# Router products on the residual sums; the last tile normalised by ScalarE and GpSimd

## The reference

```python
h = layer_norm(DEEPNORM_ALPHA * h + mix, ln1_g, ln1_b)      # mix: output projection of the mixers
# in the mixture of experts, t is h:
g_logits = t @ router_group_w + router_group_b              # 4 groups
g_idx    = top-1 of softmax(g_logits)
e_logits = t @ router_expert_w + router_expert_b            # 32 experts, 8 in a group
e_top    = top-2 of the chosen group's 8 logits, softmax over them, times the group's probability
hid = silu(t @ exp_w_gate[e]) * (t @ exp_w_up[e])           # 1024 -> 256
out = sum over the two chosen experts of weight * (hid @ exp_w_down[e])
h = layer_norm(DEEPNORM_ALPHA * h + out, ln2_g, ln2_b)
```

## Time and profile before

| | us |
|---|---|
| median of three runs | 458.99 |
| the three runs | 458.12, 458.99, 464.22 |
| profiled execution, whole time | 459.7 |
| its span | 457.5 |
| TensorE busy in the span | 417.1 (91%) |
| VectorE, ScalarE, GpSimd busy | 187.8, 107.4, 84.9 |

### The profile page before, as it was taken

The page is one execution under the profiler, slowest core; times in us unless marked ns, Lnnn a source line. Parts: engine busy times, 40 slices in busy tenths (PEclk is TensorE's granted clock), DMA queues, the critical chain, the costliest instruction groups (busy, mean ns, idle before and its releaser), DMA issues.

```text
span 457.5 us, 6658 instructions
## 1 busy us (share of the span) xinstructions
PE 417.1 (91%) x2588; PEld 283.4 (62%) x2588; DVE 187.8 (41%) x372; ACT 107.4 (23%) x175; POOL 84.9 (19%) x116
## 2 busy tenths in 40 slices
PE   7999999999999999779999999998887897889792
PEld 6888766888888888655555555554455554444330
DVE  2579322999654585762122222222121121120085
ACT  3442447741150014101111111111010010111311
POOL 2500000000000003061333322333112201012033
PEclk9999999999999999989999999999898899989997
DMA  8956322023479999396999999999999999998483
GB/s 293 278 166 215 100 92 94 1 92 94 133 283 389 413 419 381 127 398 222 416 406 409 409 408 409 411 410 409 413 410 413 408 414 414 415 414 349 152 339 142
DMA packets 44480, 139.09 MB, mean 304 GB/s; under 512 B 5288, under 2 KB 15560, under 8 KB 40359
## 3 DMA queue, kind: packets, MB, share of 16 engines
q1 hardware_dynamic: 38288, 126.89, 71.5%
q0 software_dynamic: 6144, 11.84, 7.0%
q10 hardware_dynamic: 22, 0.02, 0.0%
HBM read 134.41 MB, written 12.58 MB: 321 GB/s over the span
## 4 chain that ended last, share of the span: by engine, by line
PE 65%; DMA 18%; SPq 8%; DVE 4%; issue 2%; ACT 1%; DVEq 0%; POOL 0%; POOLq 0%
DMA wgu<-in_exp_w_up 15%; PE bank L1047 14%; PE bank L878 11%; PE bank L879 11%; PE bank L880 11%; PE bank L1066 7%; SPq L494 4%; SPq L490 2%; SPq L491 2%; PE bank L1037 2%; PE bank L1057 2%; PE bank L930 2%; DMA xg<-h_rows,x_rows 1%; DMA pair_y<-y_pairs 1%; PE bank L861 1%
## 5 line engine op out<-in xcount | busy, mean ns | idle before, releaser
L1047 PE MATMUL bank<-wgu,xTg 128*64 128x256 f32 x992 | 121.7, 401 | 19.1 <-DMA wgu<-in_exp_w_up 16.3
L1047 PEld LDWEIGHTS bank<-wgu,xTg 128*64 128x64 f32 x992 | 75.7, 144 | 56.5 <-issue 15.2
L1423 DVE TENSOR_TENSOR hid<-gated,bank 64x256 f32<-64x256 f32 x32 | 13.5, 423 | 132.7 <-ACT gated L811 132.6
L878 PE MATMUL bank<-xT_hi,w_hi 128*128 128x512 f32 x160 | 62.8, 393 | 1.4 <-DVE w_lo L1156 1.4
L879 PE MATMUL bank<-xT_lo,w_hi 128*128 128x512 f32 x160 | 62.3, 390 | 0.0
L880 PE MATMUL bank<-xT_hi,w_lo 128*128 128x512 f32 x160 | 62.3, 389 | 0.0
L652 POOL DMA_INDIRECT y_pairs<-ys,y_rows x32 | 32.3, 1011 | 161.2 <-PE bank L1037 103.8
L1066 PE MATMUL bank<-wdn,hidT 128*64 128x512 f32 x248 | 58.8, 593 | 0.9 <-issue 0.9
L811 ACT ACTIVATE gated<-bank 64x256 f32<-64x256 f32 x32 | 12.1, 377 | 161.7 <-PE bank L1047 161.7
L1142 DVE TENSOR_TENSOR w_lo<-raw,w_hi 128x2048 fp32r<-128x2048 f32 x12 | 27.5, 2290 | 33.1 <-ACT w_hi L726 32.9
L726 ACT ACTIVATE w_hi<-raw 128x2048 fp32r<-128x2048 f32 x12 | 23.0, 1920 | 59.9 <-PE bank L880 52.3
(11 more groups left out here) (237 smaller groups left out, 429.9 us busy)
## 6 DMA issues: line engine op xcount, KB each, us to landing
wgu<-in_exp_w_gate SPq DMA_DIRECT2D x31, 1024.0 KB, 16.0
wgu<-in_exp_w_up SPq DMA_DIRECT2D x31, 1024.0 KB, 21.5
wdn<-in_exp_w_down SPq DMA_DIRECT2D x31, 1024.0 KB, 21.0
raw<-in_w_in SPq DMA_DIRECT2D x9, 1024.0 KB, 5.3
raw<-in_w_out SPq DMA_DIRECT2D x4, 1024.0 KB, 5.1
pair_y<-y_pairs SPq DMA_DIRECT2D x8, 512.0 KB, 7.2
xres<-in_x SPq DMA_DIRECT2D x2, 1024.0 KB, 6.8
h_rows<-xres POOLq DMA_DIRECT2D x4, 512.0 KB, 8.2
```

The source lines that it names most:

```text
L878: pe.matmul(dst, a_hi, b_hi, start=start, stop=False)
L1047: mm = pe.matmul(psum[2 + b][BLOCK * which:BLOCK * which + BLOCK, 0:F], xTg[b][:, j, h * BLOCK:(h + 1) * BLOCK], wgu[s][:, which, k, :], s ...
```

## The change

The router's products are taken from the residual sums z and no longer from the normalised rows. With r = 1/sqrt(variance + 1e-5) and m the mean, a logit is r * (z . (g*w)) - m*r * sum(g*w) + sum(b*w) + bias. Early in the kernel VectorE scales `wr` by the norm's g (`scale_router`), TensorE transposes g and b and sums over partitions by a product with ones; the two sums stand in `across`. Each tile's mean part is put ahead in `logits`, and `take_logits` adds r times the product.

TensorE transposes each half tile of z between the output products (`turn_z`). VectorE may overwrite z by its normalised value only after that, so it normalises by half tiles, the second half one tile late. The last tile isn't normalised by VectorE: ScalarE makes (z - m) * r of each half, GpSimd multiplies by g and adds b. `last_ready` counts its halves; SP's load of `wdn_first`, TensorE's `take_first` and GpSimd's last store wait for it.

```diff
--- before.py
+++ after.py
...
@@ -515,7 +533,8 @@
             sp_.wait_ge(mixed, 2 * TT)
             load_gu(last, last, gu_in[last])
 
-            sp_.wait_ge(h1_ready, 2 * TT)
+            sp_.wait_ge(h1_ready, 2 * (TT - 1))
+            sp_.wait_ge(last_ready, 2)
             load_dn(RING, RING, dn_in[RING])
 
 
...
@@ -631,7 +653,15 @@
                     pool.wait_ge(mixed, 2 * TT)
                     for b in range(1, RING):
                         pool.memset(xg[b][:, :], 0.0).then_inc(xg_zero, 1)
-                pool.wait_ge(h1_ready, 2 * t + 2)
+                    for h in range(2):
+                        part, cols = xres[:, t, h * H:(h + 1) * H], slice(h * H, (h + 1) * H)
+                        pool.wait_ge(last_normed, h + 1)
+                        pool.tensor_tensor(part, part, ln_g[:, cols], ALU.mult).then_inc(last_scaled, 1)
+                        pool.wait_ge(last_scaled, h + 1)
+                        pool.tensor_tensor(part, part, ln_b[:, cols], ALU.add).then_inc(last_ready, 1)
+                    pool.wait_ge(last_ready, 2)
+                else:
+                    pool.wait_ge(h1_ready, 2 * t + 2)
                 pool.dma_start(h1_rows[2 * t * P:2 * (t + 1) * P, :].rearrange("(p a) h -> p (a h)", a=2), xres[:, t, :]).then_inc(h1_stored, 16)
 
             pool.wait_ge(routed, TT)
@@ -786,20 +816,22 @@
                     for j in range(CT):
                         y_split_hi(CT + j, y_sc[j][:, :])
 
-            def copy_h1T(t):
-                for n in range(2):
-                    act.wait_ge(h1_turned, 2 * t + n + 1)
-                    if t >= 2:
-
-                        act.wait_ge(logits_summed, t - 1)
-                    act.activation(h1T[t % 2][:, 4 * n:4 * n + 4, :], psum[4 + 2 * (t % 2) + n][:, :], ACT.Copy).then_inc(h1T_ready, 1)
+            def copy_zT(t, n):
+                act.wait_ge(z_turned, 2 * t + n + 1)
+                if t >= 2 and n == 0:
+
+                    act.wait_ge(logits_summed, t - 1)
+                act.activation(zT[t % 2][:, 4 * n:4 * n + 4, :], psum[4 + 2 * (t % 2) + n][:, :], ACT.Copy).then_inc(zT_ready, 1)
 
             for t in range(TT):
+                copy_zT(t, 0)
                 act.wait_ge(var_ready, t + 1)
                 act.activation(rstd[:, t:t + 1], rstd[:, t:t + 1], ACT.Sqrt).then_inc(dev_ready, 1)
-                if t >= 1:
-                    copy_h1T(t - 1)
-            copy_h1T(TT - 1)
+                copy_zT(t, 1)
+            act.wait_ge(shift_ready, 1)
+            for h in range(2):
+                part = xres[:, TT - 1, h * H:(h + 1) * H]
+                act.activation(part, part, ACT.Identity, bias=shift[:, TT - 1:TT], scale=rstd[:, TT - 1:TT]).then_inc(last_normed, 1)
 
             act.wait_ge(gdiff_ready, 2)
             act.activation(gexp[:, :, :], gexp[:, :, :], ACT.Exp).then_inc(gexp_ready, 1)
@@ -917,8 +949,19 @@
                     for j in range(CT):
                         mm = pe.transpose(psum[7][:, j * PARAMS:(j + 1) * PARAMS], par_rows[:, j * P:(j + 1) * P], ident[0:PARAMS, 0:PARAMS])
                     mm.then_inc(par_turned, 1)
+                if c == 1:
+
+                    pe.wait_ge(par_ready, 1)
+                    pe.wait_ge(ln_rows_in, 32)
+                    pe.transpose(psum[7][:, 0:2 * KT], ln_rows[:, :], ident[0:2 * KT, 0:2 * KT]).then_inc(ln_turned, 1)
+                if c == 2:
+
+                    pe.wait_ge(ones_ready, 1)
+                    pe.wait_ge(sums_ready, 1)
+                    pe.matmul(psum[7][:, 0:2 * NR], ones_f[:, :], sums[:, :, :].rearrange("p a n -> p (a n)"), start=True, stop=True).then_inc(sums_across, 1)
                 if c in (3, 4):
 
+                    pe.wait_ge(across_ready, 1)
                     pe.wait_ge(gates_in, 32)
                     for j in range(2 * c - 6, 2 * c - 4):
                         pe.wait_ge(xc_ready, j + 1)
@@ -956,39 +999,39 @@
                 pe.wait_ge(w_hi_ready, c + 1)
                 pe.wait_ge(w_lo_ready, c + 1)
 
-            def turn_h1(t):
-
+            def turn_z(t, n):
+                bank = 2 * (t % 2) + n
+                pe.wait_ge(z_ready, TT + t + 1 if n else max(t, bank) + 1)
                 if t >= 2:
-                    pe.wait_ge(h1T_ready, 2 * (t - 1))
-                for n in range(2):
-                    pe.wait_ge(h1_ready, 2 * t + n + 1)
-                    for k in range(4):
-                        mm = pe.transpose(psum[4 + 2 * (t % 2) + n][:, k * P:(k + 1) * P], xres[:, t, (4 * n + k) * P:(4 * n + k + 1) * P], ident[:, :])
-                    mm.then_inc(h1_turned, 1)
+                    pe.wait_ge(zT_ready, 2 * (t - 2) + n + 1)
+                for k in range(4):
+                    mm = pe.transpose(psum[4 + bank][:, k * P:(k + 1) * P], xres[:, t, (4 * n + k) * P:(4 * n + k + 1) * P], ident[:, :])
+                mm.then_inc(z_turned, 1)
 
             def router(t):
                 if t == 0:
-                    pe.wait_ge(router_in, 16 * 4)
-                pe.wait_ge(h1T_ready, 2 * t + 2)
+                    pe.wait_ge(wg_ready, 1)
                 for k in range(KT):
+                    if k % 4 == 0:
+                        pe.wait_ge(zT_ready, 2 * t + k // 4 + 1)
                     for q in range(2):
 
                         toks = slice(64 * q, 64 * q + 64)
-                        mm = pe.matmul(psum[t][toks, 0:NR], h1T[t % 2][:, k, toks], wr[:, k, :], start=k == 0, stop=k == KT - 1)
+                        mm = pe.matmul(psum[t][toks, 0:NR], zT[t % 2][:, k, toks], wr[:, k, :], start=k == 0, stop=k == KT - 1)
                 mm.then_inc(logits_summed, 1)
 
             for t in range(TT):
                 out_products(N_IN + 2, t, True, False)
+                if t >= 1:
+                    turn_z(t - 1, 1)
+                turn_z(t, 0)
                 out_products(N_IN + 3, t, False, True).then_inc(mixed, 1)
-                if t >= 2:
-                    turn_h1(t - 2)
-                if t >= 3:
-                    router(t - 3)
-            turn_h1(TT - 2)
-            router(TT - 3)
-            router(TT - 2)
-            turn_h1(TT - 1)
-            router(TT - 1)
+                if t == 1:
+                    router(0)
+            router(1)
+            turn_z(TT - 1, 1)
+            router(2)
+            router(3)
 
 
 
@@ -1021,6 +1064,8 @@
                                        xres[:, t, h * H:(h + 1) * H][:, cols], start=t == 0, stop=t == TT - 1)
                 mm.then_inc(first_summed, 1)
 
+            pe.wait_ge(h1_ready, 2 * (TT - 1))
+            pe.wait_ge(last_ready, 2)
             pe.wait_ge(first_hot, TT)
             take_first(0)
             take_first(1)
@@ -1238,8 +1283,30 @@
                 v.tensor_tensor(dst[0], parts[0], hi[0], ALU.subtract)
                 v.tensor_tensor(dst[1], parts[1], hi[1], ALU.subtract).then_inc(y_lo_ready, 1)
 
+            def scale_router():
+
+                v.wait_ge(ln_turned, 1)
+                link(v.tensor_copy(gb_turned[:, :, :], psum[7][:, 0:2 * KT].rearrange("p (a k) -> p a k", a=2)))
+                v.wait_ge(router_in, 16 * 4)
+                over_nr = lambda n: gb_turned[:, n, :].unsqueeze(2).to_broadcast([P, KT, NR])
+                link(v.tensor_tensor(wb[:, :, :], wr[:, :, :], over_nr(1), ALU.mult))
+                v.tensor_tensor(wr[:, :, :], wr[:, :, :], over_nr(0), ALU.mult).then_inc(wg_ready, 1)
+                v.wait_ge(wg_ready, 1)
+                link(v.tensor_reduce(sums[:, 0, :], wr[:, :, :].rearrange("p k n -> p n k"), AX, ALU.add))
+                v.tensor_reduce(sums[:, 1, :], wb[:, :, :].rearrange("p k n -> p n k"), AX, ALU.add).then_inc(sums_ready, 1)
+
+            def take_across():
+
+                v.wait_ge(sums_across, 1)
+                v.tensor_copy(across[:, 0, :], psum[7][:, 0:NR])
+                v.tensor_tensor(across[:, 1, :], psum[7][:, NR:2 * NR], rbias[:, :], ALU.add).then_inc(across_ready, 1)
+
             for s in range(N_CHUNKS - 2):
                 split_lo(s + 2)
+                if s == 0:
+                    scale_router()
+                if s == 2:
+                    take_across()
                 if s in (1, 2):
                     rg_conv(2 * s - 2)
                     rg_conv(2 * s - 1)
@@ -1267,7 +1334,8 @@
                 h, t = divmod(n, TT)
                 part = xres[:, t, h * H:(h + 1) * H]
                 v.wait_ge(mixed, n + 1)
-                link(v.scalar_tensor_tensor(out=part, in0=part, scalar=ALPHA, in1=psum[(4, 0)[h] + t][:, :], op0=ALU.mult, op1=ALU.add))
+                v.scalar_tensor_tensor(out=part, in0=part, scalar=ALPHA, in1=psum[(4, 0)[h] + t][:, :], op0=ALU.mult, op1=ALU.add).then_inc(z_ready, 1)
+                v.wait_ge(z_ready, n + 1)
                 link(v.bn_stats(stats[:, t, h, :], part))
 
             def take_moments(t, var_done):
@@ -1276,7 +1344,14 @@
 
             def take_logits(t):
                 v.wait_ge(logits_summed, t + 1)
```

(30 more changed lines are left out.)

27 lines of the change are left out of this document (24 added, 3 removed).

## The result

The changed kernel takes 466.62 us (median of 6 runs, 466.32 to 468.19), the kernel before 460.39 beside it (6 runs). The ratio is 1.0125, with a 95% interval of 1.0079 to 1.0171: slower by 1.25%, and the forecast of 466 us holds. The rise is 6.2 us by these medians, where the forecast had 7 above a median of 458.99. Four of the executions used in this document ran long beside the others of their kernel (464.94, 485.49, 534.52 and 1661.55 us) and are left out of the ratios. The profiled execution took 466.62 us with a span of 464.8, against 459.7 and 457.5 before. The start of the last residual sum, R, is now at 178.07, 4.41 us later.

What follows compares the result with a forecast made beforehand. The prediction took the kernel's end to follow the start of the first experts' products one for one; 0.25 us from (a) to (c), 5.0 from (d) and 1.7 from (e) made 6.9, forecast 466 us, range 460 to 468.5.

Steps and rivals of the forecast that it cites:

- (a): Routing chain behind the last residual sum: shorter, as VectorE no longer normalises the last tile; 3.5 us gained.
- (b): Ahead of the last output product: twenty more transposes and a router product on TensorE delay R; 3.26 us lost.
- (c): Early scaling of the router weights: one transpose and one product more on TensorE, VectorE's part hidden; 0.5 us lost.
- (d): Routing behind R: GpSimd's four half-tile operations stop VectorE steps with two SBUF inputs; 5.0 us lost.
- (e): TensorE's wait for `chosen_b`: its clock falls, slowing the eight fillers and expert 0's row sums; 1.7 us lost.
- (f): Waits for the normalised last tile by TensorE, SP's `wdn_first` load, and GpSimd's store and gathers: free.
- No stall of VectorE: Rival for the routing: GpSimd and VectorE work side by side; +1.05 us, 460 us; chance 0.15.
- The stall without the low clock: Rival: VectorE stops beside GpSimd but TensorE's clock stays full; +5.25 us, 464 us; chance 0.15.
- Not slower: Rival: inserted transposes overlap output products and GpSimd's operations fall outside the routing steps; 456 us; chance 0.08.

Runs made afterwards that it cites:

- early part alone: Kernel before plus only the early loads of g and b, their transpose, the scaled router weights and sums, all unused; ratio 1.0009.
- scale and bias turned, memsets later: Changed kernel with g and b applied to the last tile by TensorE transposes and ScalarE, not GpSimd, and memsets behind `chosen_b`; ratio 1.011.
- fillers through the wait: Changed kernel with 92 instead of 30 filler transposes on TensorE ahead of the counts; ratio 1.0176.
- scale and bias turned: Changed kernel with g and b applied to the last tile by TensorE transposes and ScalarE, without GpSimd's operations; 463.62 us, ratio 1.0088.
- the last experiment: Against the transposes-and-ScalarE kernel with memsets behind `chosen_b`: SP asks for `wdn_first` only after the last tile's store landed; 465.41 us, ratio 1.0038.

## Why the prediction was right, and where only its sum was

The profiled runs bear out one half of the frame. From the refill of `wdn` to the end the span has nearly the same length in each, within 2.1 us:

| kernel | refill starts | span | rest |
|---|---|---|---|
| before | 209.81 | 457.5 | 247.7 |
| early part alone | 210.16 | 458.9 | 248.7 |
| no operations of GpSimd | 212.53 | 460.7 | 248.2 |
| the same, memsets later | 213.36 | 461.5 | 248.1 |
| memsets earlier | 214.19 | 462.3 | 248.1 |
| scale and bias turned, memsets later | 214.23 | 462.3 | 248.1 |
| 30 transposes | 215.13 | 464.1 | 249.0 |
| store ahead of `wdn_first` | 215.66 | 465.5 | 249.8 |
| fillers through the wait | 216.32 | 464.7 | 248.4 |
| changed kernel | 216.36 | 464.8 | 248.4 |
| scale and bias turned | 216.64 | 464.7 | 248.1 |
| VectorE does the last tile | 218.79 | 467.2 | 248.4 |
| memsets in place of operations | 219.15 | 467.3 | 248.2 |

The refills of the first experts set the end, as the prediction said. The other half, that a microsecond lost ahead of the first experts is one lost at the end, fails: 3.2 us ahead of the routing became 5.3 with the 30 transposes, 0.77 at the row sums became 4.42 with scale and bias turned and the memsets later (2.4 of it by the store's wait), and row sums that were done 1.8 us sooner gave 0.04 with the fillers. Now the steps of the prediction, all measured between the two profiled runs.

**(a)** Forecast 3.5 us gained behind R, measured 8.08 less 4.67: 3.41. Right.

**(b) and (c)** Forecast 3.26 and 0.5, measured 4.41 together. The gate products are 0.86 later, 0.16 of it already at the four small transposes of the earlier trace rows, ahead of the change's first instruction on TensorE; its own part is 0.7, and 0.6 to 0.7 in the run with the early part alone, whose small transposes stood 0.09 us earlier. Between there and R lie 3.55. A transpose costs 0.107 (30 of them 3.22), so 20 are 2.1, and 1.4 is left for the router product, for which I had taken the 1.06 of a product in a row of its kind. That remainder is a difference and was not measured by itself. It also lies within what R varies: in nine profiled runs with the same early part and output projection, the changed kernel's among them, R is at 177.66 to 178.27, and at 179.43 in a tenth.

**(d)** Forecast 5.0, measured 9.42 less 4.49: 4.93. The size was right and the mechanism right for three of four stops: steps with two SBUF inputs end with GpSimd's operation. Taking the operations out gave back 4.1 us of it. But the first stop hits L1402, a step with one input, and I had reckoned such steps as running on. Of the steps with one input only the reductions and the one of one element did. The error had little effect on the sum, as I read the rows, because the chain is stopped through nearly all of the four operations whichever step is first in line. It has an effect on the remedy: with the operations gone, 0.8 us of stall stayed.

The Trainium skill, "SBUF — State Buffer", section "Who interferes with whom", lists `tensor_scalar` among the VectorE instructions that can enter a mode with both port pairs and then block against any GpSimd instruction, and says that `tensor_reduce` never contends on this chip. The rows here agree: 0.25 us free, 0.90 to 6.07 beside memsets, reductions unchanged. The prediction drew on the rule for two inputs in that section and passed over this one. The Trainium skill, "VectorE: DVE Perf Modes", section "Mode 2×_2P", splits the access in halves along its outermost dimension of more than one element, which must be even, or odd and the same for source and destination; a step of one element has no such dimension, and the one here kept its 0.16 us. By the section "Who interferes with whom" of the Trainium skill, "SBUF — State Buffer", VectorE and GpSimd exclude each other for an instruction at a time; that the waiting `tensor_scalar` lost at every change among a dozen memsets is shown by the run alone.

**(e)** This step failed. Forecast 1.7 us lost; the fillers and the start of the row sums cost 0.84 (row sums 2.69 behind `chosen_b` instead of 1.85) and the row sums 1.26. These two were forecast at 1.2 and 0.5. The 1.2 compared fillers that begin 0.9 us behind `chosen_b` with row sums that begin 1.55 behind its end; from that end the fillers begin at 0.45 (192.90 less 192.45). The 0.5 was set at less than half of the 1.1 us of expert 1's products, because fillers had run ahead. But the products of expert 1, slow in the kernel before, ran at full clock and gave 1.10 back, and 0.47 more came back between the gather of expert 1's rows and its products. Net 0.62 with the 0.09 of the gather. What failed is the premise that the fall of the clock is an extra. The kernel before already has one, at expert 1, and I charged the new one without crediting the old, though both stood in the earlier trace rows. The profiled run with fillers shows it from the other side: full clock at the row sums, low clock at expert 1, the same refill to 0.04 us.

**(f)** Forecast free, and it is, but with little in hand. In the changed kernel the store is issued at 190.09 and the gather starts at 201.40 behind the row table. With the row table 1.5 us earlier (VectorE does the last tile) the store held the gather, and again with scale and bias turned and the memsets later. What I called 1 MB in an idle stretch of the DMA engines more than doubled the store's time: 3.3 us alone, 7.0 to 8.6 beside the load.

**The sum.** At the refill: 4.41 - 3.41 + 4.93 + 0.62 = 6.55, as the rows have it; 0.75 more came behind it, spread over the end, within what the rest varies in the table (247.7 to 249.8). The forecast had 6.9. (b) and (c) were 0.65 too small and (e) 1.08 too large. So the right time owes something to luck: two errors of opposite sign.

**The rivals.** "No stall of VectorE" is refuted by the four steps. "The stall without the low clock" is refuted in its words (clock 0.50), yet its arithmetic, with no net cost of the clock, was the nearer one for that step. "Not slower" needed the inserted work below 3.0 us; 30 transposes alone were 3.22.

**What stays open.** Why the clock falls in one kernel and not in another after the same wait, and why the gather took 6.1 to 6.4 us in some runs and 6.9 to 7.4 in others; both enter into what a delay ahead of the routing costs (3.2 us became 5.3 with the 30 transposes: 1.2 in the gather, 0.7 in the products of expert 1). How much of the differences between two profiles is chance: the kernel before alone took 457.67 to 464.11 us in 23 executions on one chip, and each kernel has one profile, so parts of less than 1 us are not shown to belong to the change. What VectorE waited for at 205.8 us in the last experiment.

## What to carry to other kernels

Work that is taken off the critical engine and given to GpSimd is not free beside VectorE: look at what VectorE executes in that stretch. Here steps with two SBUF inputs stopped beside GpSimd's `tensor_tensor` and not beside its memsets, and a `tensor_scalar` of 128x8 stopped beside both; reductions and a `tensor_scalar` of 128x1 ran on. Count the former as stopped for as long as GpSimd is busy. Before charging a fall of TensorE's clock, look where the kernel already has one; it may only move. And when a chain is shortened, look for the DMA whose landing was hidden behind it, here a store that a prefetch delays.

## What the runs showed of the hardware that I had not expected

- A run of GpSimd memsets stops a VectorE `tensor_scalar` (128x8, fp32, SBUF) until the last of them: a pair takes 0.25 us free, 0.90 beside the last two of five (the kernel with scale and bias turned), 6.07 beside the last dozen of sixteen. A `tensor_scalar` of 128x1 isn't stopped (0.16), nor are reductions or steps with two inputs. In two kernels the same pair, 0.89 us, was stopped from a moment when GpSimd was only issuing a store.
- A 512 KB store from GpSimd's queue landed in 3.3 us with no load beside it, in 2.9 where the load had been asked for 6.4 us earlier (the kernel with more memsets), and in 7.0 to 8.6 (five kernels) beside a 1 MB load from SP's, asked for 0.2 us ahead of it.
- After the same wait of 1.17 us TensorE's granted clock stayed at 1.00 in one kernel and was at 0.61 and 0.54 in the next, with the same instructions of TensorE around it, 0.31 us later in time. With the fall came 1.2 us at the row sums.
